# First projection block of a hybrid attention and mixture-of-experts layer: x loaded in column halves, its chunks computed one by one, the second block's load moved ahead of the small vectors

## The reference, cut to what matters

```
h    = rms_norm(x, g_attn)
proj = h @ w_in          # 1024 x 4896: q | kv | gates | fox q,k,v | forget | merge logits
...                      # compressed, selected and window attention; forgetting attention
x = x + (merged mixers) @ w_out
x = x + moe_ffn(rms_norm(x, g_mlp))   # 32 experts, top 4, clamped SwiGLU, 3 matrices of 1024 x 1024 each
```

## Time and profile before

| | |
|---|---|
| median of 3 runs | 1139.85 us (1139.14 to 1141.07) |
| profiled execution, its own time | 1138.89 us |
| its span in the profile | 1137.1 us |
| PE busy | 1092.3 us, 96% of the span |
| DVE, ACT, POOL busy | 409.6, 179.3, 90.3 us |
| moved by DMA | 438.88 MB, mean 386 GB/s |

### The profile page before, as it was taken

One profiled execution on the slowest core, in us unless ns is written; L12 is line 12 of the kernel. 1 busy time (PEld: TensorE's weight loads), 2 busy tenths in 40 slices (PEclk: granted clock), 3 DMA queues, 4 the chain that ended last, 5 costly groups with the idle time before them and its releaser, 6 DMA issues.

```text
span 1137.1 us, 14543 instructions
## 1 busy us (share of the span) xinstructions
PE 1092.3 (96%) x5733; PEld 513.9 (45%) x5733; DVE 409.6 (36%) x973; ACT 179.3 (16%) x370; POOL 90.3 (8%) x89
## 2 busy tenths in 40 slices
PE   8999999999999999999999999999999999999997
PEld 7888899843333333333333333333333333333333
DVE  5883666532223222223322222222222222222222
ACT  6546664400000000000000000000000000000000
POOL 2226447000000000000000000000000000000000
PEclk9999999999989999999999999999999999999999
DMA  9955724999999999999999999999999999999996
GB/s 309 344 195 220 225 75 147 425 405 421 428 418 412 427 429 428 427 429 428 429 428 429 428 429 427 429 428 429 429 428 429 426 429 427 430 427 428 426 428 280
DMA packets 50572, 438.88 MB, mean 386 GB/s; under 512 B 6786, under 2 KB 12998, under 8 KB 25062
## 3 DMA queue, kind: packets, MB, share of 16 engines
q1 hardware_dynamic: 50470, 438.23, 93.1%
q10 hardware_dynamic: 64, 0.14, 0.0%
HBM read 437.30 MB, written 1.05 MB: 385 GB/s over the span
## 4 chain that ended last, share of the span: by engine, by line
PE 65%; DMA 34%; issue 0%; DVE 0%; ACT 0%; POOL 0%; POOLq 0%; SPq 0%; DVEq 0%
PE bank L1939 35%; DMA ring<-in_w_e_up_dram 18%; DMA ring<-in_w_e_gate_dram 12%; PE bank L1912 3%; PE bank L1960 3%; DMA ring<-in_w_e_down_dram 3%; PE bank L1928 2%; PE bank L1533 2%; PE bank L1701 1%; PE bank L1702 1%; PE bank L1703 1%; PE bank L1980 1%; PE bank L1542 1%; PE bank L1544 1%; PE bank L1543 1%; PE bank L1536 1%
## 5 line engine op out<-in xcount | busy, mean ns | idle before, releaser
L1939 PE MATMUL bank<-ring,heads 128*64 128x512 f32 x3004 | 679.0, 599 | 14.8 <-DMA ring<-in_w_e_gate_dram 13.1
L1939 PEld LDWEIGHTS bank<-ring,heads 128*64 128x64 f32 x3004 | 204.2, 137 | 421.0 <-issue 376.5
L1463 DVE TENSOR_TENSOR x<-x,bank 128x512 f32<-128x512 f32 x124 | 79.8, 684 | 144.9 <-PE bank L1960 144.9
L1411 DVE TENSOR_SCALAR heads<-bank 128x512 f32<-128x512 f32 x32 | 22.1, 691 | 289.5 <-PE bank L1939 289.5
L907 ACT ACTIVATE work<-bank 128x256 f32<-128x256 f32 x32 | 12.3, 383 | 492.3 <-PE bank L1973 492.3
L708 POOL TENSOR_TENSOR x<-x,heads 128x256 f32<-128x256 f32 x2 | 1.4, 729 | 912.1 <-ACT heads L941 912.1
L1960 PE MATMUL bank<-heads,work 64*128 64x512 f32 x248 | 72.3, 641 | 0.0
L409 POOL TENSOR_TENSOR w_lo<-ring,w_hi 128x1024 fp32r<-128x1024 f32 (+1 forms) x35 | 65.3, 1894 | 53.8 <-ACT w_hi L731 53.8
L731 ACT ACTIVATE w_hi<-ring 128x512 fp32r<-128x512 f32 (+2 forms) x82 | 57.6, 732 | 25.2 <-PE bank L1790 7.3
L1912 PE MATMUL bank<-work,xn 128*128 128x128 f32 x480 | 58.5, 275 | 0.0
L1912 PEld LDWEIGHTS bank<-work,xn 128*128 128x128 f32 x480 | 56.0, 192 | 0.0
(11 more groups left out here) (323 smaller groups left out, 976.3 us busy)
## 6 DMA issues: line engine op xcount, KB each, us to landing
ring<-in_w_e_gate_dram SPq DMA_DIRECT2D x61, 2048.0 KB, 30.6
ring<-in_w_e_up_dram SPq DMA_DIRECT2D x61, 2048.0 KB, 31.7
ring<-in_w_e_down_dram SPq DMA_DIRECT2D x60, 2048.0 KB, 31.8
ring<-in_w_in_dram SPq DMA_DIRECT2D x8, 2048.0 KB, 10.2
ring<-in_w_e_down_dram SPq DMA_DIRECT2D x8, 1024.0 KB, 17.5
spare<-in_w_e_gate_dram SPq DMA_DIRECT2D x2, 2048.0 KB, 15.7
ring<-in_w_out_dram SPq DMA_DIRECT2D x2, 2048.0 KB, 8.1
ring<-in_w_e_up_dram SPq DMA_DIRECT2D x4, 1024.0 KB, 7.1
```

The source lines that it names most:

```text
L1411: nc.vector.tensor_scalar(e_g, banks[1][:, :], LIMIT, None, ALU.min).then_inc(g_made, 1)
L1463: ins = nc.vector.tensor_tensor(x[:, t, 512 * h:512 * h + 512], x[:, t, 512 * h:512 * h + 512], bank67[:, j % 2, :], ALU.add)
L1939: last = mm(bank[C * half:C * half + C, :], lhs(kk), kept_row[half] if kept else w[:, k, 512 * half:512 * half + 512], start=(kk == 0 and ...
```

## The change

- **SP.** x is loaded by halves of 512 columns, each with a semaphore of its own. The order is x first halves of tile 0 and 1, chunks 0, 1, 2-3, x second halves of both tiles, chunks 4-5, 6-7. The load of `kw` stands ahead of the small vectors instead of behind them. `q` stays behind them.
- **ACT.** The gain rows go to a place of their own in `work`, so that their load waits for nothing. The order of `xT_hi` and `w_hi` follows the new order on PE. The squares wait for both halves.
- **DVE.** A memset of `xn` for the fill-in matmuls stands first. `keep_xT` takes the place of `keep_hT_tile` for this block; `xT_lo` and `w_lo` are interleaved by half.
- **PE.** Eight matmuls of `xn` that wait for DVE's memset replace four of `ident`; the first column half of both tiles is transposed ahead, with the gain rows between; five fill-in matmuls follow instead of four. Then the three products of a chunk come together, chunk by chunk for both tiles; the second halves are transposed behind chunk 1. `chunk_used` is counted as the chunks end.

```
-            load_x(0)
+            load_x(0, 0)
+            load_x(1, 0)
             load_kv(0, 1, kv_in[0])
             load_kv(1, 2, kv_in[1])
-            load_x(1)
             load_kv(2, 4, kv_in[2])
+            load_x(0, 1)
+            load_x(1, 1)
             load_kv(4, 6, kv_in[3])
             load_kv(6, 8, ring_in[slot_of["kv"]])
...
+            load("kw", BLOCKS[1][1])
             sp.wait_ge(vrow_set, 1)
...
-            load("kw", BLOCKS[1][1])
             load("q", BLOCKS[2][1])
...
-            act.wait_ge(vrow_set, 1)
-            act.dma_start(vrow[R_GA:R_GA + 8, :], ...).then_inc(gain_rows_in, 16)
+            act.dma_start(gain_rows, ...).then_inc(gain_rows_in, 16)
...
             keep_high_tile(0, 0)
             keep_high_lead(0)
+            keep_high_tile(1, 0)
+            for k in (1, 2, 3):
+                keep_high_lead(k)
             keep_high_tile(0, 1)
-            keep_high_lead(1)
-            keep_high_tile(1, 0)
-            keep_high_lead(2)
             keep_high_tile(1, 1)
-            for k in (3, 4, 5):
+            for k in (4, 5):
                 keep_high_lead(k)
...
+            nc.vector.memset(xn[:, 0, 0:P], 1.0).then_inc(warm_set, 1)
...
+            keep_xT(0, 0)
+            keep_xT(1, 0)
+            keep_low_tile(0, 0)
             keep_low_chunks(0, (0,))
+            keep_low_tile(1, 0)
+            keep_low_chunks(0, (1, 2))
+            keep_xT(0, 1)
+            keep_xT(1, 1)
+            keep_low_chunks(0, (3,))
+            keep_low_tile(0, 1)
+            keep_low_tile(1, 1)
+            keep_low_chunks(0, (4, 5, 6, 7))
...
+            pe.wait_ge(warm_set, 1)
+            fill_in(8)
             pe.wait_ge(consts_made, 1)
+            turn_x(0, 0, range(0, 2))
             pe.wait_ge(gain_rows_in, 16)
-            nc.tensor.transpose(TB[0][:, 0:KD], vrow[0:KD, :], ident[0:KD, 0:KD]).then_inc(gain_turned, 1)
+            nc.tensor.transpose(TB[0][:, 0:KD], gain_rows, ident[0:KD, 0:KD]).then_inc(gain_turned, 1)
+            turn_x(0, 0, range(2, 4))
+            turn_x(1, 0)
+            fill_in(5)
...
                 by_high(0, (0,))
-                turn_tile(1)
+                by_low(0, 0)
                 by_high(0, (1,))
-                by_low(0, 0)
-                by_high(0, (2, 3))
-                by_high(1, (0, 1, 2, 3))
-                for ks in ((4, 5), (6, 7)):
+                by_high(1, (0,))
+                by_low(1, 0).then_inc(chunk_used, 1)
+                by_high(1, (1,))
+                by_low(0, 1)
+                by_low(1, 1).then_inc(chunk_used, 1)
+                turn_x(0, 1)
+                turn_x(1, 1)
+                for k in range(2, KD):
                     for t in range(NT):
-                        by_high(t, ks)
-                for k in range(KD):
+                        by_high(t, (k,))
                     for t in range(NT):
                         last = by_low(t, k)
```

More of the change, by code:

```diff
@@ L214, in build @@
         b_gate = sm_(32)
+        gain_rows = work[0:KD, 2176:2304]
         diag_r = work[:, 2048:2304].rearrange("p (t q) -> p t q", t=NT)
@@ L240, in build @@
         logits = work[:, 1472:1536].rearrange("p (t e) -> p t e", t=NT)
-        x_in = [sem(f"x_in{t}") for t in range(NT)]
+        x_in = [[sem(f"x_in{t}_half{j}") for j in range(2)] for t in range(NT)]
+        warm_set = sem("warm_set")
         vec_in, small_in, ebias_in, bdown_in, out_sent = map(sem, (
@@ L721, in square_rows @@
                 nc.scalar.activation(squares, x[:, t, :], ACT.Square, accum_out=ss[:, t:t + 1]).then_inc(squared, 1)
[L722 to L723 removed]
+            act.dma_start(gain_rows, a["g_attn"][0].rearrange("(r n) -> r n", r=8)).then_inc(gain_rows_in, 16)
             def keep_high(j):
@@ L734, in keep_high_tile @@
             def keep_high_tile(t, j):
-                act.wait_ge(hT_made, 2 * t + j + 1)
+                act.wait_ge(hT_made, 2 * j + t + 1)
                 k, q = slice(4 * j, 4 * j + 4), slice(P * t, P * t + P)
@@ L755, in _ @@
             for t in range(NT):
-                act.wait_ge(x_in[t], 16)
+                for j in range(2):
+                    act.wait_ge(x_in[t][j], 16)
                 square_rows(t, heads[:, 2048 + D * t:2048 + D * t + D])
@@ L966, in keep_hT_tile, with keep_xT @@
                                             col(vcol[:, gain_col + 4 * j:gain_col + 4 * j + 4], P), ALU.mult).then_inc(hT_made, 1)
+            nc.vector.memset(xn[:, 0, 0:P], 1.0).then_inc(warm_set, 1)
+            def keep_xT(t, j):
+                dve.wait_ge(xn_turned, 2 * j + t + 1)
+                nc.vector.tensor_tensor(hT[:, 4 * j:4 * j + 4, P * t:P * t + P],
+                                        (PJ, S)[t][j][:, :].rearrange("p (k q) -> p k q", k=4),
+                                        col(vcol[:, R_GA + 4 * j:R_GA + 4 * j + 4], P), ALU.mult).then_inc(hT_made, 1)
             dve.wait_ge(gain_turned, 1)
@@ L970, in _, with keep_low_tile @@
             dve.wait_ge(gain_kept, 1)
[L971 to L979, removed]
+            def keep_low_tile(t, j):
+                q, ks = slice(P * t, P * t + P), slice(4 * j, 4 * j + 4)
+                dve.wait_ge(hT_made, 2 * j + t + 1)
+                dve.wait_ge(hT_hi_made, 2 * j + t + 1)
+                nc.vector.tensor_tensor(xT_lo[:, ks, q], hT[:, ks, q], xT_hi[:, ks, q], ALU.subtract).then_inc(hT_lo_made, 1)
             def keep_low_chunks(b, chunks=range(KD)):
@@ L1499, in _, with turn_x, fill_in @@
             mm = nc.tensor.matmul
[L1501 to L1506, removed]
-                    last.then_inc(xn_turned, 1)
+            def turn_x(t, j, ks=range(4)):
+                pe.wait_ge(x_in[t][j], 16)
+                for k in ks:
+                    c = P * (4 * j + k)
+                    last = nc.tensor.transpose((PJ, S)[t][j][:, P * k:P * k + P], x[:, t, c:c + P], ident[:, :])
+                if ks.stop == 4:
+                    last.then_inc(xn_turned, 1)
+            def fill_in(n):
+                for _ in range(n):
+                    mm(TB[1][:, 0:P], xn[:, 0, 0:P], xn[:, 0, 0:P], start=True, stop=True)
+            pe.wait_ge(warm_set, 1)
+            fill_in(8)
             pe.wait_ge(consts_made, 1)
-            for _ in range(4):
-                mm(OB[0][:, 0:P], ident[:, :], ident[:, :], start=True, stop=True)
+            turn_x(0, 0, range(0, 2))
             pe.wait_ge(gain_rows_in, 16)
-            nc.tensor.transpose(TB[0][:, 0:KD], vrow[0:KD, :], ident[0:KD, 0:KD]).then_inc(gain_turned, 1)
[L1513 to L1519, removed]
+            nc.tensor.transpose(TB[0][:, 0:KD], gain_rows, ident[0:KD, 0:KD]).then_inc(gain_turned, 1)
+            turn_x(0, 0, range(2, 4))
+            turn_x(1, 0)
+            fill_in(5)
             def project(i, name, n, between={}):
@@ L1570, in by_high @@
                         pe.wait_ge(hi_made, k + 1)
-                        pe.wait_ge(hT_lo_made, 2 * t + k // 4 + 1)
+                        pe.wait_ge(hT_lo_made, 2 * (k // 4) + t + 1)
                         for h in (xT_hi, xT_lo):
```

12 lines of the change are left out of this document (3 added, 9 removed).

## The result

The changed kernel is slower. Its median is 1145.80 us (1144.26 to 1146.78, 5 runs), that of the kernel before, run beside it, 1139.57 us (1138.58 to 1141.07, 5 runs). The ratio is 1.0053, 95% interval 1.0041 to 1.0064: 6.2 us more, where 1.85 less was forecast. The profiled execution took 1144.55 us with a span of 1142.8, which is 5.7 more than before.

The account below looks back on a forecast made before the run. PE's program was taken to bound the kernel up to 190 us, then the expert-weight stream at 428 GB/s. A first-block gain of 1.85, from 1139.85, gave 1138.0 us; range 1136.6 to 1139.9.

Parts of the forecast that it names:

- PE ahead of the first product: PE's fill-ins and transposes before the first block: first product at 8.3 us, 0.45 later than now, clock as before.
- the block: First block on PE: runs through without waits, ends at 20.1 us against 21.74; gain 1.65, with earlier clock 2.05, taken 1.85.
- The rival of more than forecast: Clock rises 2 to 3 us earlier, first block starts at 7.3: gain 2.4 to 2.6, time 1137.3; chance 22%.
- More and smaller DMAs: Loads of x and `kv`: 2 us fixed per DMA in series would end `kv` at 16.4, about 1139.9; judged unlikely.
- The small vectors: Small loads behind `kw`: landed by 18.4 us at most, PE asks at 20.1, so hidden by 1.7 us or more.
- Later blocks: Loads behind the first block: come up to 1.3 us earlier as the queue's hole at 8 to 13 fills; otherwise little lost.
- PE's program sets the time up to 190 us: Before the weight stream: PE's work sets the time, so its first-block gain starts the stream earlier by the same amount.
- Slower, 10%: SP's issue held behind `kw`: last small vector lands at 24.9, 3.2 us later than 21.74; time 1143.0, chance 10%.
- Nothing arrives at the end: Stream's start does not move: something of fixed time before it, or x or `kv` 1 to 2 us late; 1139.9, 10%.
- The sum: Whole kernel: profiled run 1138.89 minus 1.85 gives 1137.0; median 1139.85 minus 1.85 gives 1138.0.

Follow-up runs that it names:

- the eight columns late: Changed kernel with only the eight last columns of `kw` loaded behind the 17 small loads, its 280 columns still ahead: 1141.67 us, ratio 1.0015.
- `q` ahead too: Changed kernel with the load of `q` also moved ahead of the 17 small loads on SP, directly behind `kw`: 1143.64 us, ratio 1.0034.
- the queue put right: Changed kernel with the 17 small loads issued by ACT, so that `q` follows `kw` directly on SP: 1138.03 us, ratio 0.9989.
- the queue's part alone: Kernel before, engine order kept, with `kw` and `q` directly behind `kv` on SP and the small loads on ACT: 1138.95 us, ratio 0.9991.

## Why the prediction was wrong

- **PE ahead of the first product, and the block.** The times were 0.26 and 0.46 off, the first of them by luck. It was put at 8.3, as the end of slow fill-ins. The clock had risen by 6.8 us, though, and not at 8.0 (six transposes from 5.47 take 0.22 us each, ten records of fill-ins from 6.80 only 0.13), so the fill-ins ended at 8.10. PE then stood for 0.46 us: `xT_lo`(0,0), put at 7.9, was there at 8.4. An early clock and a late DVE nearly cancelled. From 8.56 on the block ran through, and its end at 20.56 makes a gain of 1.18 instead of 1.65 to 2.05. The rival of more than forecast fell in this profile. Its mechanism is there in others: with `kw` behind the small loads, the eight columns late and `q` ahead too, the transposes at 5 us were fast already (0.12 each), and the first product came at 7.80, 7.91 and 7.69.
- **More and smaller DMAs.** By the Trainium skill's rule on transfers of 1 MiB or more (DMA: Bandwidth & Descriptors, Rules for kernel authors) the finer pieces would have come late. They did not: PE has no wait on a chunk, and 8 to 13 us ran at 390 GB/s. (What the pages say against cutting a transfer is said of halves by partition, and their 2 us were fitted to DMAs issued by GpSimd; the prediction carried both over to halves by column issued by SP.) What two more DMAs cost is SP's time, which the working left out: with `kw` in its old place all that follows them is issued 1.4 us later, and that alone eats the block's gain.
- **The small vectors.** Their time was right in its result (PE at L1621 waits for nothing) and wrong in its working. SP was held for some 5 us (3.67 where the three DMAs of `kw` and `q` took 2.30 in the earlier trace rows, and 2.62 where a small one took 0.38; less their own issue), though by bytes 2.7 MB were outstanding, less than the 4 behind which the issue had been held before. The run with the eight columns late shows the mistake: the hold follows the pieces handed over rather than their bytes, and `kw`'s second DMA is 1024 of them in 32 KB. The small issues ended 5.3 us later than the 13.1 of the working, past the 3.3 from which the rival made the vectors late. They were in time because the last one, issued at 17.95, had landed by 20.56: 2.6 us, not the 5.3 assumed, on a queue that had run dry.
- **Later blocks: the step that failed.** It said that they "come up to 1.3 us earlier" and that even if `fk` comes no earlier, "little is lost". `q` was never moved past the small loads, and these now started 4.9 us later (9.10 instead of 4.18, and slower in the first), so `q` was issued some 5 us later and `fk` 3.5. The working priced every queue that `kw` was moved past, and not what was then behind it on the same queue. The 5.27 us that ACT waits for `fk` in the earlier trace rows were read as slack. They were slack of ACT, not of the transfer: the table puts the transfer level with PE's path.
- **PE's program sets the time up to 190 us.** True of the trace read, with 0.2 us to the other path. PE's busy 57.65 of 58 us could not show how near the other path was.
- **Slower, 10%.** The place (SP's issue) was right, the victim was not: the rival looked at the vectors, which only the run with `q` ahead too makes late. At 1143.0 it lies nearest to the result, and still 2.8 short of it, since it has neither the late blocks nor the lower clock behind the wait.
- **Nothing arrives at the end.** Its mechanism, a transfer that stands before the stream, was the right one to fear; in the run with `kw` behind the small loads it does more than swallow the gain (the stream starts 1.56 later).
- **The sum.** The term "minus 1.85" was +5.7 in the profile: -1.2 for PE's block, which the wait at `fk` swallowed; at the stream +3.6 for `fk`'s landing and +0.7 for the lower clock behind it; +1.4 for the stretch at 228 us. With the queue put right the term is -1.3 at the stream, and the median 1138.03. That 1138.0 had been forecast for the change as it stood is in part luck: the gain was put at 1.85, and by the ratio it is 1.3, from a median of the kernel before that was 0.3 lower than the one the forecast started from.

What stays open: how many pieces SP can have outstanding, what the bytes add, and whether the tiny pieces count by their number or by the time that they take to move; whether the 0.9991 of the queue's part alone is a gain; what makes the clock rise earlier in one profile than in the next; and what sets off the lower clock near 228 us. Each kernel has one profile, while its executions lie up to 5.0 us apart, so differences of some tenths between two profiles carry little.

## What to carry to other kernels

When a load is moved ahead on a queue, price what is left behind it and not only it: each later load of that queue moves by the whole issue time of what it now stands behind, holds included. Before a gain on the bounding engine is booked, ask of the next waits of the others by how much their transfers are early for that engine, since several paths can be level: here two were, within 0.2 us. Many tiny loads belong on an engine that is idle at that time, not between two big blocks, where they took 7 us of issue during which the DMA engines ran dry.

## What the runs showed of the hardware

- An issue can be held by the pieces handed over before it rather than by their bytes. The second small load started at 6.03 us with no `kw` ahead, at 8.57 behind `kw`'s 280 columns (1024 pieces, 1120 KB), and at 11.77 with its 8 columns ahead too (1024 pieces more, 32 KB): the 32 KB cost 3.2 us and the 1120 KB, with their own issue of 0.72, cost 2.5.
- PE waits of 3.40, 3.33 and 2.40 us at `fk` were each followed by a first product of 0.77 us and a pitch of 0.43, the lower level of 1.2 GHz; waits of 1.82 and 1.18 us at the same place were not. Fifteen unused matmuls in the wait kept the level.
- With PE at work from 1.13 us on in the same program, the rise to 2.4 GHz came before 5 us in some profiles (transposes of 0.12 us each from 4.96 on with `kw` behind the small loads) and only near 6.8 in others (0.22 each from 5.47 on in the changed kernel).
- DMAs of 256 and 512 KB, queued back to back with `kw` behind them, moved 390 GB/s at 8 to 13 us, against 366 in the full stretch of the earlier trace rows. By the 232 GB/s of 0 to 8 us, some 1.3 of the 1.95 MB moved there were theirs (an estimate), the rest `kw`'s. Their own size did not slow them.
